# A two-block kernel on one core: the decay matrices of the state-space branch built from one broadcast row per head, and the gate tiles shared out anew between the branch steps

## The reference, cut to what matters

```python
    xdt = xf * dtf[..., None]
    cs = jnp.cumsum(dtf * a.astype(jnp.float32).reshape(ng, r), axis=2)
    mask = jnp.tril(jnp.ones((CHUNK, CHUNK), dtype=bool))
    seg = cs_h[..., :, None] - cs_h[..., None, :]
    decay = jnp.exp(jnp.where(mask, seg, -jnp.inf))
    cb = jnp.einsum('bctgn,bcsgn->bcgts', cf, bf)
    y_intra = jnp.einsum('bcgts,bcgrts,bcsgrp->bctgrp', cb, decay, xdt)
    ...
    g = jax.nn.sigmoid(gates.reshape(bsz, seq, N_BRANCH, D_MODEL))
    merged = (g[:, :, 0] * (y_a @ w_up_a) + g[:, :, 1] * (y_b @ w_up_b)
              + g[:, :, 2] * (y_c @ w_up_c) + g[:, :, 3] * (y_d @ w_up_d))
    return merged @ w_out
```

## Time and profile before

| | us |
|---|---|
| median of 3 runs | 2931.82 |
| lowest, highest | 2931.29, 2933.14 |
| the profiled execution, its own time | 2933.65 |
| its span in the trace | 2931.8 |
| PE busy | 2774.6 (95%) |
| DVE busy | 1635.0 (56%) |
| ACT busy | 1133.5 (39%) |

### The profile page before, as it was taken

How to read it: one execution, slowest core, us unless ns; L and a number is a source line. 1 busy time by engine, 2 the same in 40 slices (tenths; PEclk the granted TensorE clock), 3 DMA queues, 4 the chain that set the end, 5 groups by cost and what they waited for, 6 DMA issues and landing times.

```text
span 2931.8 us, 39437 instructions
## 1 busy us (share of the span) xinstructions
PE 2774.6 (95%) x16254; PEld 2413.4 (82%) x16254; DVE 1635.0 (56%) x2663; ACT 1133.5 (39%) x1743; POOL 0.3 (0%) x5
## 2 busy tenths in 40 slices
PE   7999899999998998999989998999989999899898
PEld 6988899988898996888864786888868888688898
DVE  6653677656447776555551356555565444655654
ACT  6453444445434443223232343222232232344443
POOL 0000000000000000000000000000000000000000
PEclk9997999999899998999989999999999999999999
DMA  5532557544235774444431013444434444320554
GB/s 182 176 118 75 170 183 228 185 139 144 94 108 190 228 223 130 150 148 145 145 108 50 22 66 114 139 149 151 144 110 142 151 146 148 115 66 30 174 183 133
DMA packets 114050, 403.17 MB, mean 138 GB/s; under 512 B 12368, under 2 KB 15568, under 8 KB 113744
## 3 DMA queue, kind: packets, MB, share of 16 engines
q1 hardware_dynamic: 113872, 400.66, 42.3%
HBM read 399.56 MB, written 1.05 MB: 137 GB/s over the span
## 4 chain that ended last, share of the span: by engine, by line
PE 91%; DVE 4%; ACT 3%; issue 2%; DMA 0%; SPq 0%; DVEq 0%; ACTq 0%
PE psum L533 25%; PE psum L534 25%; PE psum L535 25%; PE psum L834 2%; PE psum L861 1%; PE psum L961 1%; PE psum L969 1%; PE psum L801 1%; PE psum L803 1%; ACT whi L1039 1%; PE psum L802 1%; ACT L1067 1%; DVE wlo L1417 1%; PE psum L529 0%; PE psum L927 0%
## 5 line engine op out<-in xcount | busy, mean ns | idle before, releaser
L533 PE MATMUL psum<-HHI,whi 128*128 128x256 f32 (+1 forms) x3456 | 1124.9, 325 | 57.5 <-DVE HLO L1483 32.4
L534 PE MATMUL psum<-HLO,whi 128*128 128x256 f32 (+1 forms) x3456 | 1115.7, 323 | 0.0
L535 PE MATMUL psum<-HHI,wlo 128*128 128x256 f32 (+1 forms) x3456 | 1114.9, 323 | 0.0
L1417 DVE TENSOR_TENSOR wlo<-wring,whi 128x1024 fp32r<-128x1024 f32 x590 | 707.9, 1222 | 410.3 <-ACT whi L1039 408.0
L1039 ACT ACTIVATE whi<-wring 128x1024 fp32r<-128x1024 f32 x590 | 607.0, 1053 | 465.8 <-PE psum L535 445.5
L533 PEld LDWEIGHTS psum<-HHI,whi 128*128 128x128 f32 x3456 | 667.9, 193 | 122.2 <-issue 64.3
L534 PEld LDWEIGHTS psum<-HLO,whi 128*128 128x128 f32 x3456 | 667.8, 193 | 48.9 <-issue 1.4
L535 PEld LDWEIGHTS psum<-HHI,wlo 128*128 128x128 f32 x3456 | 667.1, 193 | 48.3
L533 PE MATMUL psum<-HIDHI,whi 128*128 128x256 f32 (+1 forms) x1056 | 357.2, 338 | 0.0
L534 PE MATMUL psum<-HIDLO,whi 128*128 128x256 f32 (+1 forms) x1056 | 357.2, 338 | 0.0
L535 PE MATMUL psum<-HIDHI,wlo 128*128 128x256 f32 (+1 forms) x1056 | 357.1, 338 | 0.0
(11 more groups left out here) (280 smaller groups left out, 2125.0 us busy)
## 6 DMA issues: line engine op xcount, KB each, us to landing
wring<-ffn_in SPq DMA_DIRECT2D x264, 512.0 KB, 4.2
wring<-mod_w SPq DMA_DIRECT2D x144, 512.0 KB, 4.3
wring<-ffn_out SPq DMA_DIRECT2D x96, 448.0 KB, 3.5
wring<-w_proj SPq DMA_DIRECT2D x66, 512.0 KB, 4.2
wring<-w_gate SPq DMA_DIRECT2D x64, 512.0 KB, 3.7
wring<-ffn_out SPq DMA_DIRECT2D x48, 512.0 KB, 4.2
wring<-w_up SPq DMA_DIRECT2D x20, 512.0 KB, 3.3
wring<-w_out SPq DMA_DIRECT2D x16, 512.0 KB, 3.3
```

The costliest lines, as they stand in the source:

```text
L533: mm(out_, w[0], a[0], start=start, stop=False)
L534: mm(out_, w[0], a[1], start=False, stop=False)
L535: return mm(out_, w[1], a[0], start=False, stop=stop)
L1417: TTN(wlo[:, i, :], wring[:, raw_slot(tag, k), :], whi[:, i, :].bitcast(F32), ALU.subtract).then_inc(sem("weights_lo"), 1)
```

## The change

Three things are edited.

`sg`: TensorE makes one product per head, which broadcasts the running sum of the head over 128 rows (256 columns, 8 partitions of contraction), and neither subtracts nor masks. The negative running sum is transposed beside the step sizes (two more small transposes at `dtt`), so that DVE has it as one value per partition. DVE adds it and clamps at 0 while it copies out of PSUM (two instructions per head, 256 and 128 columns), ACT takes the exponential in place in SBUF, and DVE multiplies by C·B as before. The mask is now a matrix of 0 and 1, `tri_up` (128 more columns of constants), with which DVE multiplies C·B once per group.

The order on DVE: two masks, the segments of heads 0 and 1, then in turn the segment of head h+2 and the product of head h.

`GATE_LOTS`: `gkt` 4 to 6, `gkv` 2 to 1, `yo` 2 to 4, `up` 5 to 2. The sum stays 32.

```diff
-for _name, _n in (("la", 1), ("gkt", 4), ("gkv", 2), ("go", 2), ("gss", 1), ("rs", 4), ("ro", 1), ("rss", 2),
-                  ("xt", 4), ("cb", 1), ("yo", 2), ("yss", 3), ("up", 5)):
+for _name, _n in (("la", 1), ("gkt", 6), ("gkv", 1), ("go", 2), ("gss", 1), ("rs", 4), ("ro", 1), ("rss", 2),
+                  ("xt", 4), ("cb", 1), ("yo", 4), ("yss", 3), ("up", 2)):
...
 (ssd_pe)
-                pe.wait_ge(*done("ssd_dt", l))
+                pe.wait_ge(*done("ssd_cs", l))
                 pe.wait_ge(*bank_free(("dtt", l)))
                 bank = bank_of(("dtt", l))
-                for tt in range(TT):
-                    last = pe.transpose(bank[:, tt * SSD_HEADS:(tt + 1) * SSD_HEADS],
-                                        d2["DX"][0:SSD_HEADS, 0, tt * P:tt * P + P], ident[0:SSD_HEADS, 0:SSD_HEADS])
+                for i, row in enumerate((d2["DX"], d2["NCS"])):
+                    for tt in range(TT):
+                        at = (TT * i + tt) * SSD_HEADS
+                        last = pe.transpose(bank[:, at:at + SSD_HEADS], row[0:SSD_HEADS, 0, tt * P:tt * P + P], ident[0:SSD_HEADS, 0:SSD_HEADS])
...
                 for h in range(SSD_HEADS):
                     pe.wait_ge(*bank_free(("sg", l, h)))
-                    bank = bank_of(("sg", l, h))
-                    for st in range(TT):
-                        a, n = st * SEQ, SEQ - st * P
-                        mm(bank[:, a:a + n], head_row(SSD_HEADS, h, P), CS[:, st * P:SEQ], start=True, stop=False)
-                        mm(bank[:, a:a + n], NCS[:, st * P:st * P + P], head_row(SSD_HEADS, h, n), start=False, stop=False)
-                        last = mm(bank[:, a:a + P], ident, cst("mask_up"), start=False, stop=True)
-                    last.then_inc(*mark("filled", ("sg", l, h)))
+                    mm(bank_of(("sg", l, h))[:, 0:SEQ], head_row(SSD_HEADS, h, P), CS, start=True, stop=True).then_inc(*mark("filled", ("sg", l, h)))
...
 (ssd_act)
-                    act.wait_ge(*done("filled", ("sg", l, h)))
-                    bank = bank_of(("sg", l, h))
-                    A(d1["L"][:, h, :], bank[:, 0:CAUSAL], ACT.Exp).then_inc(*freed(("sg", l, h), "ssd_l", (l, h)))
+                    act.wait_ge(*done("ssd_seg", (l, h)))
+                    A(d1["L"][:, h, :], d1["L"][:, h, :], ACT.Exp).then_inc(*mark("ssd_l", (l, h)))
...
 (ssd_dve)
+                def segment(h):
+                    v.wait_ge(*done("filled", ("sg", l, h)))
+                    bank = bank_of(("sg", l, h))
+                    TS(d1["L"][:, h, 0:SEQ], bank[:, 0:SEQ], small["DTT"][:, TT, h:h + 1], 0.0, ALU.add, ALU.min)
+                    TS(d1["L"][:, h, SEQ:CAUSAL], bank[:, P:SEQ], small["DTT"][:, TT + 1, h:h + 1], 0.0, ALU.add,
+                       ALU.min).then_inc(*freed(("sg", l, h), "ssd_seg", (l, h)))
+                def masked(g):
+                    v.wait_ge(*done("ssd_cb", (l, g)))
+                    cb = d1["CB"][:, g, :].rearrange("p (b t) -> p b t", b=3)[:, 0:3:2, :]
+                    TTN(cb, cb, cst("tri_up").unsqueeze(1).to_broadcast([P, 2, P]), ALU.mult).then_inc(*mark("ssd_mask", (l, g)))
+                for g in range(2):
+                    masked(g)
+                segment(0)
+                segment(1)
                 for h in range(SSD_HEADS):
-                    v.wait_ge(*done("ssd_cb", (l, h // 4)))
+                    if h + 2 < SSD_HEADS:
+                        segment(h + 2)
+                    if h % 4 == 0:
+                        v.wait_ge(*done("ssd_mask", (l, h // 4)))
                     v.wait_ge(*done("ssd_l", (l, h)))
                     TTN(d1["L"][:, h, :], d1["L"][:, h, :], d1["CB"][:, h // 4, :], ALU.mult).then_inc(*mark("ssd_w", (l, h)))
```

More of the change, by code:

```diff
@@ L69 @@
 _at = 0
-for _name, _w in (("ident", P), ("ones", P), ("heads64", P), ("mask_low", P), ("mask_up", P), ("chunk_up", P),
+for _name, _w in (("ident", P), ("ones", P), ("heads64", P), ("mask_low", P), ("mask_up", P), ("chunk_up", P), ("tri_up", P),
                   ("cos2", SEQ), ("sin2", SEQ),
@@ L333, in build @@
         small = carve([("FX", 1, SEQ), ("FA", 1, SEQ), ("CC", 1, SEQ), ("NCC", 1, SEQ), ("NM", 1, 16), ("RS", 1, 16),
-                       ("RC", 1, 16), ("DTT", TT, SSD_HEADS), ("GLR", 1, SEQ)], m1["end"] + 8192)
+                       ("RC", 1, 16), ("DTT", 2 * TT, SSD_HEADS), ("GLR", 1, SEQ)], m1["end"] + 8192)
         g1 = carve([("GX", 2, SEQ), ("GA", 2, SEQ), ("B", 2, SEQ), ("ND", 2, SEQ), ("EB", 2, SEQ), ("EI", 2, SEQ),
@@ L770, in ssd_pe @@
             def ssd_pe(l):
-                CS, NCS = d2["CS"][0:SSD_HEADS, 0, :], d2["NCS"][0:SSD_HEADS, 0, :]
+                CS = d2["CS"][0:SSD_HEADS, 0, :]
                 gates_pe(l, "xt")
-                pe.wait_ge(*done("ssd_dt", l))
+                pe.wait_ge(*done("ssd_cs", l))
                 pe.wait_ge(*bank_free(("dtt", l)))
                 bank = bank_of(("dtt", l))
-                for tt in range(TT):
-                    last = pe.transpose(bank[:, tt * SSD_HEADS:(tt + 1) * SSD_HEADS],
-                                        d2["DX"][0:SSD_HEADS, 0, tt * P:tt * P + P], ident[0:SSD_HEADS, 0:SSD_HEADS])
+                for i, row in enumerate((d2["DX"], d2["NCS"])):
+                    for tt in range(TT):
+                        at = (TT * i + tt) * SSD_HEADS
+                        last = pe.transpose(bank[:, at:at + SSD_HEADS], row[0:SSD_HEADS, 0, tt * P:tt * P + P], ident[0:SSD_HEADS, 0:SSD_HEADS])
                 last.then_inc(*mark("filled", ("dtt", l)))
@@ L1166, in gla_act @@
                 A(g1["EK"], g1["ND"], ACT.Exp, scale=1.0 / GLA_TAU).then_inc(*mark("gla_e", (l, 2)))
-                gate_step(l, "gkt", 2)
-                gate_step(l, "gkt", 3)
+                for i in range(2, len(GATE_LOTS["gkt"])):
+                    gate_step(l, "gkt", i)
                 gate_step(l, "gkv")
@@ L1682, in ssd_pre @@
                 bank = bank_of(("dtt", l))
-                v.tensor_copy(small["DTT"], bank[:, 0:TT * SSD_HEADS].rearrange("p (t h) -> p t h", t=TT)).then_inc(*freed(("dtt", l)))
+                v.tensor_copy(small["DTT"], bank[:, 0:2 * TT * SSD_HEADS].rearrange("p (t h) -> p t h", t=2 * TT)).then_inc(*freed(("dtt", l)))
                 dve.wait_ge(*done("free", ("dtt", l)))
@@ L1926, in constants @@
     put("mask_up", np.where(r <= c, 0.0, NEG))
+    put("tri_up", (r <= c).astype(np.float32))
     put("chunk_up", ((r <= c) & (r // CHUNK == c // CHUNK)).astype(np.float32))
```

## The result

| | before | after |
|---|---|---|
| median of the runs, us | 2931.56 (4 runs) | 2863.58 (4 runs) |
| lowest, highest | 2930.67, 2933.14 | 2862.42, 2865.19 |
| profiled execution, own time | 2933.65 | 2864.3 |
| its span | 2931.8 | 2862.5 |

The ratio is 0.9767, with a 95% interval of 0.9755 to 0.978. The forecast was 2859 (2852 to 2868): the time lies in the range, 4.6 us above the point and 0.6 above the forecast's own range of 2855 to 2863. The sum promised 72.6 us, and the spans of the two traces differ by 69.3.

What follows compares the result with a forecast made beforehand. PE, busy 95% of the span, was taken as the bound. 58.9 + 0 + 11.5 + 2.8 - 0.4 - 0.2 = 72.6 us off the median 2931.82 gave 2859 us, range 2852 to 2868 for 8 in 10.

Steps and rivals of the forecast that it cites:

- sg, products: At sg, 48 products per layer become 8 of 0.54 us, 4.3 us a stage; gain 58.9 us over both layers.
- It just meets them: At sg, DVE returns the banks of segments 0, 1 and 2 just when PE wants them, at T + 4.6, 5.2, 5.7.
- The clock around it: Clock falls again towards the end of sg; the lots behind lose 1.76 us as now; gain 0, bounds 0 and 3.5.
- rival 1: The clock does not fall in the short sg stage; lots behind gain 1.76 us per layer, 2855.7 us; chance 0.22.
- sg, DVE: DVE's new 10 us per layer at sg cost nothing; segments 0.67 us, products 0.52, eighth ssd_w at T + 13.2.
- Rival 2: DVE paces sg: segment, exponential and product do not overlap, banks come late; 2.9 us per layer, 2865 us; chance 0.14.
- The cover at yo: Two more lots at yo cover DVE's work with 4 us of slack; with two lots PE would wait 1.6 us.
- gkt: Two more lots fill PE's idle time before L694, gaining 11.5 us; the clock holds behind, 2.8 more, both layers.
- Rival 3: The gkt lots only move the wait, as their parts come late; 11.5 and 2.8 us not gained, 2873.5 us; chance 0.06.
- up, and the small things: Fewer up lots cost 0 before the merge (bound 0.4 us); extra dtt transposes cost 0.4 for both layers, constants 0.2.
- The rule weighed in the prediction: Skill's rule ties clock loss to PE idle gaps, so sg would keep full clock; the prediction said the trace disagrees.

Runs made afterwards that it cites:

- full_height: The changed kernel with its eight sg products contracting over all 128 partitions (120 of them zero) in place of 8; 2860.37 us, ratio 0.9754.
- the second profile: The changed kernel profiled once more with no edit; 2860.29 us (one run).
- lots_only: The kernel before, with its old sg of 48 products, given only the new table of gate lots; 2919.17 us, ratio 0.9958.
- gkt_order: The changed kernel with ACT preparing the second gkt lot before waiting for gla_b, and DVE making gla_kez after two low parts, not four; 2858.81 us, ratio 0.9748.
- best_fh: The changed kernel with both full-height sg products (128 partitions) and the two moved gkt steps; 2852.77 us, ratio 0.9728.
- old_sg_full: The kernel before, with the 32 thin sg products of each layer contracting over 128 partitions instead of 8; 2892.65 us, ratio 0.986.

## Why the prediction was right, and where it missed

**sg, products.** Right in kind, and near in size by luck: 4.56 and 4.46 us in place of the 4.3. The price of 0.54 us belongs to a product that stands beside others of another height; of eight in a row only the first takes it, and the next five take 0.43, the lower bound. Six products are 0.48 us under the sum's 3.24. The last two bring that back and more, with 1.80 us in place of 1.08, as their banks come from DVE 0.65 us apart and the clock falls just before the eighth. "It just meets them" was a sum without slack.

**The clock around it.** This is the mis-sized term. The fall was foretold with its place, and the full clock of rival 1 did not come, except where the products were made full height. But the loss was set equal to that of before, 1.76 us in a layer. Measured against the 11.68 us of `full_height`, the four lots lost 2.46 and 2.58 us, and the end of the stage ran at 0.50 too: with the clock held, stage and lots would be 4.15 + 11.68 = 15.83 us, and they were 18.70 and 18.73, so the clock cost 2.9 us in a layer. The clock came back 5.6 and 5.9 us after dense work began, where the earlier trace rows had given 4.0. One reading of this delay was taken for a constant; the second profile, with 3.4 and 6.8 us at 0.50 in two layers of one execution, shows that it isn't. With the shorter one the lots lose 1.5 us (13.18 less 11.68), near the forecast. Over both layers the term accounts for 2.25 of the 3.3 us by which the traces miss the sum.

**sg, DVE.** Segments every 0.65 us (0.67 taken), products every 0.46 (0.52), the last one ready at T + 12.4 (13.2), T being 224.94 here: the pipeline ran as worked out. Rival 2 was true of the last two products only.

**The cover at yo.** Wrong, though it moved no number: the two lots are not needed there. The step that failed is "PE asks for the eighth `ssd_w`" at the start of the `yo` products.

**gkt.** Right, wait and all: 0.97 us inside the lots (0.9), L694 without idle time and at the full clock, 0.60 before L714 (0.6). 7.11 and 6.79 us in place of 7.16. `lots_only` measures it alone, 13.4 us against 14.3. Rival 3 has fallen.

**up, and the small things.** No wait before the merge, DVE done 1.2 us ahead of it (0.5 to 1.5). The two more small transposes of a layer cost 0.13, by the stretch in which they lie. For the 0.2 us of the constants there is no measurement: the `gkt` lots began at 142.59 before, at 142.75 here, and at 142.36 in `gkt_order`, which has the same constants.

**What the sum did not hold.** 0.8 us outside the changed stages. The four executions beside the result differ by 2.8 us among themselves, and the one of the second profile lies 2.1 under the lowest of them, so no run could show a cause.

**The rule weighed in the prediction.** The Trainium skill (TensorE: Matmul & The Clock Gate, HAM oscillation — how this bites in real kernels) ties the loss to idle gaps. The trace after disagrees once more at `sg`, 0.84 and then 0.50 with PE busy 1.00. At `gkt` and at L856 it fits in kind: with 0.97 us in place of 6.83 the clock held, and behind 3.78 us it fell in eight traces of fourteen.

## What to carry to other kernels

A long stretch at half the clock with PE busy is a sign to look at the shape of the products before their number: here zero rows and a taller operand alone gave 41.7 us, where the whole change gave 68. To fill a wait with independent lots is worth their full length, once it is seen that their own operands come before the chain that is waited for. Whether a cover is needed is asked of the last consumer, head by head, and not of the first instruction of the stage; and a delay of the clock that was read once or twice is a range, not a constant.

## What the runs showed of the hardware

- Products over 8 of 128 partitions lower the granted clock with PE busy 1.00. The same products over 128 partitions hold 1.00 (`full_height`, `best_fh`, `old_sg_full`). The fall came 3.2 to 4.2 us after the first of them in the four layers of the two profiles of the changed kernel, and 3.0 to 5.4 us over the twelve stages of all kernels that have the short thin stage.
- A float32 product of 256 columns has a pace of 0.43 us over 8 partitions as over 128, at the full clock in both cases. What costs time is a change of height between neighbours: by the estimate above 0.2 us each, 2.53 us for a mixed head and 1.76 for one of equal heights.
- The time at 0.50 behind the same short stage was 3.4 us or 6.8, in one execution and the same program; that is 1.4 us of time between the two.
- The same idle time of 3.78 us before the same products cost the clock in eight traces and not in six; it was worth 0, 1.7 or 2.5 us.
